# A boundary's two sums of squares, taken in split form and scheduled around it anew, in a two-layer decoder trunk

## The reference, cut to what matters

```python
def rmsnorm(x, g):
    y = xf * lax.rsqrt(jnp.mean(xf * xf, axis=-1, keepdims=True) + EPS)
    return y * g
...
h = rmsnorm(x, p['norm_pre'][0])
x = x + 0.5 * rmsnorm(swiglu(h, ...[0]), p['norm_post'][0])
h = rmsnorm(x, p['norm_pre'][1])
m = mixer(h, ...)          # w_in, RG-LRU heads | GLA heads, w_out
x = x + rmsnorm(m, p['norm_post'][1])
h = rmsnorm(x, p['norm_pre'][2])
x = x + 0.5 * rmsnorm(swiglu(h, ...[1]), p['norm_post'][2])
```

## Time and profile before

| | |
|---|---|
| median of three runs | 2171.91 us (2171.76 to 2172.25) |
| the profiled execution, its time | 2172.07 us |
| the profiled execution, its span | 2169.8 us |
| TensorE busy (matmul) | 2151.7 us, 99% of the span |
| VectorE, ScalarE, GpSimd busy | 1442.9, 1291.6, 707.0 us |
| granted TensorE clock, mean | 0.998 |

### The profile page before, as it was taken

The page is one execution under the profiler, slowest core; times in us unless marked ns, Lnnn a source line. Parts: engine busy times, 40 slices in busy tenths (PEclk is TensorE's granted clock), DMA queues, the critical chain, the costliest instruction groups (busy, mean ns, idle before and its releaser), DMA issues.

```text
span 2169.8 us, 40918 instructions
## 1 busy us (share of the span) xinstructions
PE 2151.7 (99%) x17060; PEld 2128.4 (98%) x17060; DVE 1442.9 (66%) x1897; ACT 1291.6 (60%) x1987; POOL 707.0 (33%) x711
## 2 busy tenths in 40 slices
PE   8999999999999999999999999999999999999997
PEld 8999999999999999999999999999999999999997
DVE  7554857778996658845584558577699867576454
ACT  7634657657785646643564356576577765575433
POOL 4012511625645224501250124024265533152111
PEclk9999999999999999999999999999999999999999
DMA  7555555445554455555555555554465544555553
GB/s 236 162 164 162 166 174 156 146 145 168 165 158 136 148 183 158 167 164 165 166 165 164 166 165 162 170 157 144 140 182 156 156 137 154 180 165 159 162 168 122
DMA packets 102390, 350.70 MB, mean 162 GB/s; under 512 B 11392, under 2 KB 16512, under 8 KB 102208
## 3 DMA queue, kind: packets, MB, share of 16 engines
q1 hardware_dynamic: 100976, 346.83, 52.5%
q10 hardware_dynamic: 1232, 1.27, 0.2%
HBM read 343.19 MB, written 4.87 MB: 160 GB/s over the span
## 4 chain that ended last, share of the span: by engine, by line
PE 96%; DVE 1%; POOL 1%; issue 1%; ACT 1%; DMA 0%; SPq 0%; DVEq 0%; POOLq 0%; ACTq 0%
PE psD L488 92%; PE psM L568 1%; POOL ssum L1578 1%; PE psM L609 0%; DVE val L1447 0%; PE psM L679 0%; DVE wl L1122 0%; DMA x<-in_xT 0%; PE psM L642 0%; PE psM L684 0%; POOL hidl L1778 0%; PE psM L694 0%; PE psS L506 0%; PE psM L548 0%; PE psM L546 0%
## 5 line engine op out<-in xcount | busy, mean ns | idle before, releaser
L488 PE MATMUL psD<-hh,wh 128*128 128x288 f32 x3712 | 1106.8, 298 | 3.5 <-DMA ident<-in_ident 2.4
L488 PE MATMUL psD<-hl,wh 128*128 128x288 f32 x3712 | 1095.0, 295 | 0.0
L488 PE MATMUL psD<-hh,wl 128*128 128x288 f32 x3712 | 1091.5, 294 | 0.0
L1122 DVE TENSOR_TENSOR wl<-raw,wh 128x1024 fp32r<-128x1024 f32 (+1 forms) x656 | 826.5, 1260 | 119.1 <-ACT wh L785 118.5
L785 ACT ACTIVATE wh<-raw 128x1024 fp32r<-128x1024 f32 (+1 forms) x656 | 672.4, 1027 | 99.5 <-DMA raw<-in_w_gu 48.4
L488 PEld LDWEIGHTS psD<-hh,wh 128*128 128x128 f32 x3712 | 695.6, 187 | 9.7 <-issue 6.2
L488 PEld LDWEIGHTS psD<-hh,wl 128*128 128x128 f32 x3712 | 698.9, 188 | 0.0
L488 PEld LDWEIGHTS psD<-hl,wh 128*128 128x128 f32 x3712 | 696.9, 188 | 1.5
L1778 POOL TENSOR_TENSOR hidl<-hid,hidh 128x288 fp32r<-128x288 f32 x176 | 214.6, 1219 | 907.8 <-ACT hidh L1071 907.8
L488 PE MATMUL psD<-hidh,wh 128*128 128x288 f32 x1408 | 417.5, 297 | 0.4 <-POOL hidl L1778 0.4
L488 PE MATMUL psD<-hidl,wh 128*128 128x288 f32 x1408 | 415.4, 295 | 0.0
(11 more groups left out here) (221 smaller groups left out, 1506.7 us busy)
## 6 DMA issues: line engine op xcount, KB each, us to landing
raw<-in_w_gu SPq DMA_DIRECT2D x352, 512.0 KB, 3.5
raw<-in_w_d SPq DMA_DIRECT2D x128, 448.0 KB, 3.2
raw<-in_w_in SPq DMA_DIRECT2D x80, 512.0 KB, 3.5
raw<-in_w_d SPq DMA_DIRECT2D x64, 512.0 KB, 3.6
raw<-in_w_out SPq DMA_DIRECT2D x32, 512.0 KB, 3.6
gates<-in_w_ax SPq DMA_DIRECT2D x4, 512.0 KB, 4.5
S<-in_st_gla SPq DMA_DIRECT2D x4, 512.0 KB, 4.4
out_gla_s<-S SPq DMA_DIRECT2D x4, 512.0 KB, 5.4
```

The source lines that it names most:

```text
L488: mm = e.matmul(out, w[:, kt * P:(kt + 1) * P], t[:, kt, :], start=(kt == 0 and part == 0), stop=(kt == KT - 1 and part == 2))
L1122: e.tensor_tensor(wl[u % RING][:, 0:width], raw[u % RING][:, 0:width], wh[u % RING][:, 0:width].bitcast(F32), ALU.subtract).then_inc(lo_re ...
```

## The change

The boundary of group 0 after its output projection (st = 1, g = 0, once in each layer) leaves the quick form, and its second sum moves from slot 18 to slot 17 in `pace`. Its first stays at slot 3.

```diff
     def is_quick(l, st, g):
-        return (st, g) in ((0, 1), (1, 0)) or is_final(l, st)
+        return (st, g) == (0, 1) or is_final(l, st)
...
         if s.kind == "wout" and s.g == 0:
-            return 3, 18, 1
+            return 3, 17, 1
```

## The result

The changed kernel takes 2177.66 us, median of 10 runs (2177.45 to 2177.86), against 2171.86 us before (10 runs). The ratio is 1.0027 with a 95% interval of 1.0018 to 1.0035: it is 5.8 us slower. I had forecast 2173.3 us and a range up to 2175.2, and had given slower by more than 0.2% a chance of 0.05. Three executions on record are far off all others (one of the kernel before at 3726 us, two of `quick_end_17` at 7428 and 11966 us), and no reading rests on them. The profiled execution took 2177.45 us, its span is 2175.2 us, so 2.25 us lie around it, as before; the 5.4 us are inside the trace.

A forecast was written before the change was run, and what follows sets the result against it. TensorE, busy every moment of win, was taken to bound the kernel. Per layer, -0.44 us saved and +1.1 us lost at ffn 3 make +0.7, twice +1.4: 2173.3 us from a median of 2171.91, range 2171.0 to 2175.2.

The forecast's parts named there:

- TensorE's saving: Two sums a layer go from fp32 (0.49 us) to split (0.27 us): 0.44 us less per layer, 0.88 in all.
- The first sum: Slots 3 to 5: the later guess makes VectorE 1.56 us late at its product; TensorE's loss taken as 0.
- bounds of 0 and 0.9 us a layer: TensorE's loss from the first sum: 0.9 if all of 1.56 remains at slot 12, 0 if two thirds are won back.
- a cover of 0.65 us at win 15: The lateness of VectorE's `wl` for win 15 that TensorE could bear before losing time: 0.65 us.
- The reason that I gave for winning it back: VectorE's operations slowed beside GpSimd would fall partly into its new wait; a replay of slots 8 to 12 left 0.3 us.
- two readings that agreed: ScalarE's late root and VectorE's own queue each put VectorE 1.6 to 1.8 us late at slot 8.
- The second sum: Slots 18 to 19: the guess delays the last logarithms, VectorE's difference comes 2.3 us later, ffn 3 loses 1.1 us.
- a drain behind the table load: In the second guess's chain: the skill's drain of about 1.38 us makes ffn 3 lose 2.5 us; 2176.1, chance 2 in 100.
- The added work at slot 17: ScalarE's ACTIVATE (0.43 us) and VectorE's subtraction (0.46 us) lie before points where these engines wait anyway: costed at nothing.
- both stretches stall: Rival: the first stretch also stalls, adding 0.5 to 0.9 us a layer: 2174.3 to 2175.1; chance 0.25.
- The slower rival: Slots 5 to 8: the root's 3.2 us of lateness all reach win 15, 3.2 us net a layer: 2178.3; chance 0.05.
- the prediction's own signs of being wrong: TensorE waiting near win 14 or 15 (599 to 603 us), or for `ssl` at slot 19, or nowhere.

The follow-up runs named there:

- `quick_end_17`: The kernel before, both sums in fp32, with the second sum at slot 17 instead of 18: 2171.74 us.
- `split_2_17_guess_19`: The changed kernel with its first sum from slot 2, GpSimd adding four squares a slot ahead of it, second guess at slot 19, refinement at 20: 2171.07 us.
- `first_split_start_2`: The kernel before with only the first sum split, from slot 2, GpSimd adding four squares a slot ahead of it; second in fp32 at slot 18: 2171.33 us.
- `first_split`: The kernel before with only the first sum split (slot 3, product at 5), the second in fp32 at slot 18: 2174.58 us.
- `quick_4_18`: The kernel before, both sums in fp32, with the first one slot later, at slot 4: 2174.51 us.
- `second_split`: The kernel before with only the second sum split (slot 17, product at 19), the first in fp32 at slot 3: 2173.76 us.
- `split_work_only`: The kernel before with ScalarE's rounding and VectorE's remainder added at slots 3 and 17, their results unused: 2171.89 us.
- `split_16_product_19`: The changed kernel with `ssum` split for the second sum at slot 16 instead of 17, the products still at 5 and 19: 2175.96 us.

## Why the prediction was wrong

**TensorE's saving: right.** 0.88 us forecast; 0.82 us measured where nothing stalls (`split_2_17_guess_19`), 0.40 for half of it (`first_split_start_2`).

**The first sum: this step failed.** The prediction took 0 for its stall, out of bounds of 0 and 0.9 us a layer. It had VectorE 1.56 us late at slot 7 and a cover of 0.65 us at win 15, and then let two thirds of the lateness be won back before win 15. The trace shows 1.41 us at slot 7 and 1.56 us at slot 12, and the loss is 1.1 us at win 15 and 0.2 at win 17; `first_split` prices the whole at (2.7 + 0.44) / 2 = 1.6 us a layer, with 0.25 more at ffn 3. The reason that I gave for winning it back was wrong. The time that VectorE loses beside GpSimd was to fall in part into its new wait for the root; there was no such wait, and the lost time only moved to other instructions. My estimate from VectorE's rows of layer 0, each against the time of the same operation alone, is 3.0 us before and 2.8 us after from refinement to product, and 4.3 and 4.5 us from there to the `wl` of win 15. The upper bound was the plain difference of two numbers that I had, 1.56 - 0.65, and I took the other end. The loss is 1.1 and not that bound's 0.9, since TensorE was 0.17 us early at win 0 in this execution, so that VectorE's lateness against it was 1.7 us. Nor was win 15 the only thin place: the `wl` of win 17 ended 1.06 us ahead of its unit before, that of win 15 1.00. I was also half wrong on who makes VectorE late. I worked out two readings that agreed, ScalarE's late guess and VectorE's own queue; `quick_4_18` has ScalarE on time and loses 1.3 us a layer all the same, so VectorE's queue suffices. In the changed kernel, too, VectorE has no wait noted from 571.04 to past the `wl` of win 17, so ScalarE's lateness stops it nowhere there; whether it acts by shifting GpSimd's additions isn't separated.

On this stretching the Trainium skill ("GPSIMD Engine Reference", Specifications) says that GpSimd shares its SBUF interfaces with VectorE, in contention with VectorE's instructions with two SBUF inputs. The rows agree: 2.59 us beside an add of 2.46 us, 1.36 without one.

**The second sum: right in mechanism, size a little low.** 1.1 us a layer at ffn 3; `second_split` gives (1.86 + 0.44) / 2 = 1.15 us. In the changed kernel the step there is 1.3 us in layer 0, where VectorE's scan (L1316) waits 0.26 us that it doesn't wait in `second_split`, and 1.1 us in layer 1. The row decided rightly against a drain behind the table load: the next ACTIVATE stands 0.01 us behind it again (the load ends at 624.66, the next starts at 624.67), and the stretch is 3.84 us.

**The added work at slot 17: costed at nothing, wrong in this kernel.** Alone it costs nothing (`split_work_only`). But the cover that I named, VectorE's wait for the logarithms, lies behind the remainder in its order, and TensorE's product in slot 19 waits for the remainder. With VectorE late from the first sum, `ssl` came 0.5 us too late for TensorE at the end of win 19, and since the guess, the logarithms and `wl` of ffn 3 all hang on that product, the wait is not covered by anything. `split_16_product_19` wins 1.6 us on its own chip's measure by taking it away, 0.8 a layer, and the trace of the changed kernel shows 0.7 lost there. It is the 1.2 us that the sums' single prices didn't explain, and a little more: at ffn 3 the pair adds nothing, 1.3 us there against 0.25 and 1.15 in the two single kernels.

**The rivals.** What happened is nearest to "both stretches stall", whose price of 2174.3 to 2175.1 lacked the wait for `ssl` and the loss at win 17: 2.5 us more. The slower rival gave 2178.3 and the right sign, by a lateness of 3.2 us at win 15; there it was 1.56 us. Its size was nearly met by other terms, not by its mechanism. No rival let the first stall feed a third one. Yet the prediction's own signs of being wrong named both: TensorE waiting near win 15, and for `ssl` at slot 19.

**The sum as it should have been**, a layer: -0.44, first sum 1.1 + 0.2, `ssl` 0.7, ffn 3 1.3: 2.9 us, twice 5.8, as measured (the changed trace has 2.95 in layer 0 and 2.7 in layer 1).

What stays open: what the scan of layer 0 waited 0.26 us for, and what ScalarE's lateness does by way of GpSimd.

## What to carry to other kernels

When a step on a saturated engine is moved from its one gap into its full stretch, take its lateness as kept until a row shows an idle piece that can absorb it; here 1.41 us at slot 7 were 1.56 us at slot 12, against a cover of 0.65 us that was known. A later producer is cheap or dear by what stands behind its consumer in that engine's order: the same product at the same slot cost 1.15 us a layer with the guess ahead of the logarithms, and nothing with it behind them. Where two covers lie one after the other on one engine, cost the second with the first one's loss in place, since late work spends it.

## What the runs showed of the hardware that I had not expected

One multiplication of VectorE over 128 x 1152 elements with two operands took 1.36 us alone and 2.59 us beside an addition of GpSimd over 128 x 576, which itself took 2.46 us. The trace of the kernel before has such pairs too: `hl` of one tile took 0.51 us at 582.77 and 1.70 us at 586.26, beside an addition of 2.50 us. So which of VectorE's instructions lies beside GpSimd moves the time of one by more than 1 us, while in slots 4 to 12 the sum of these losses changed by 0.2 us or less in each of the two parts that I compared.
